# Latent attention: who multiplies the odd items' probabilities by the reciprocals of their sums

## The chip, the cores and the metric

The kernel is one program on one core of a Trainium2 chip. It runs a whole two-block network on 512 tokens of width 1024 in float32. The metric is the device time of one execution in microseconds (us); the median of three executions of the kernel before is 2576.47 us (2576.43 to 2576.89).

## The reference, cut to what matters

The network is a chain of mixers and feed-forward layers. The change touches one of them only, the latent attention (MLA) of the second block, and in it only the softmax:

```python
def chunk_causal_attention(q, k, v):          # q, k: 16 heads of 96, v: 16 heads of 64
    ...
        sc = jnp.einsum('bqhd,bkhd->bhqk', qi, k) * scale
        mask = key_chunk[None, :] <= q_chunk[:, None]
        p = jax.nn.softmax(jnp.where(mask, sc, -jnp.inf), axis=-1)
        return jnp.einsum('bhqk,bkhd->bqhd', p.astype(v.dtype), v)
    ...
```

## The kernel before, in words

Each engine has its own program, and semaphores order them against each other. TensorE runs one long queue of matmuls through the whole network; ScalarE and VectorE prepare operands and read results; GpSimd has little to do.

The latent attention is cut into 32 items (`MLA_ITEMS`). An item is two heads (e = 0, 1) by one block of 128 queries; its width w is the number of keys it sees: 128, 256, 384 or 512 columns. Items come in pairs of one width, an even and an odd one; item m of the pair s = m // 2. By `mla_block` the widths of the pairs 0 to 15 are 128, 256, 384, 512, then 256, 384, 512, 128 three times over. One item goes through these stages, each once for e = 0 and once for e = 1 where it says so:

1. TensorE, `scores` (L2808 and L2813, two matmul lines, both heads): scores into PSUM.
2. VectorE, `maxima` (L2910, once per head): adds the mask, writes the masked scores to SBUF (`mla_soft`) and takes the row maxima; L2917 turns the maxima into the bias of the exponentials and increments `item_max`.
3. ScalarE, `exponentials` (L2883, once per head): the exponentials in place, with their row sums.
4. VectorE, `normed` (L2922, the reciprocals of both sums, then L2924 once per head): probabilities in place, which increments `item_normed`.
5. TensorE, `turn` (L2829): transposes w / 128 blocks of each head into PSUM.
6. ScalarE, `copy` (L2873 or L2876): the transposed probabilities to SBUF.
7. TensorE, `values` (L2844): probabilities times values.

The order on each engine is written out by hand. In step s, TensorE does turn(2s-4), scores of the pair s, turn(2s-3), values(2s-5), values(2s-4) (`pe_mla_step`). VectorE does normed(2s-2), maxima(2s), maxima(2s+1), normed(2s-1) (`dve_mla_soft`), and after that in some steps a piece of other work: two quarter splits of a weight block (L373) in steps 6 and 7, the rope part of a key (two L2738) in steps 7 and 8, the low part of a projection operand (L712) in steps 12 and 14. ScalarE does copy(n-4), exponentials(n-2) (`act_mla_soft`). TensorE may overwrite the score banks of a pair only when the maxima of the pair before are read (the wait for `item_max` in `scores`).

GpSimd's last work before the softmax is `pool_mla` (L2727: 16 additions of squares), its next is `pool_pairs(0)` in the feed-forward layer behind the attention. The statistics (`mla_stat`) of kind 3, the reciprocals, have two slots, one for even and one for odd items.

Of the kernel before, what the change touches and what calls it, by code (L numbers as in the profile page):

```python
# [20 lines left out]
ALU = mybir.AluOpType  # L21
# [136 lines left out]
def build(nc, A, stop=None):  # L158

    with ExitStack() as ctx:  # L160
        sems = {}

        def sem(name):
            if name not in sems:
                sems[name] = ctx.enter_context(nc.semaphore(name))
            return sems[name]
# [2258 lines left out]
        def mla_soft(n, e):  # L2425
            a = (26 + n % 6 * 2 + e) * SEQ
            return arena[:, a:a + SEQ]

        def mla_stat(kind, n, e, count=1):
            c = (4, 12, 20, 24)[kind] + n % (4, 4, 2, 2)[kind] * 2 + e  # L2430
            return stats[:, c:c + count]
# [7 lines left out]
        def k_plain(j, lo=0, hi=P):  # L2439
            return tile(12 + j, lo, hi)  # L2440
# [32 lines left out]
        def pair_squares(s):  # L2473
            return hn_tile(s % 3)
# [243 lines left out]
        def pool_mla(pool):  # L2718

            for s in range(16):  # L2720
# [5 lines left out]
                other = rope_squares(s // 2, s % 2) if s < 8 else krope_sq()  # L2726
                pool.tensor_tensor(pair_squares(s), pair_squares(s), other, ALU.add).then_inc(sem("pair_sq"), 1)  # L2727

        def dve_key(dve, j, parts=("plain", "rope")):
            by = mla_rq(j)  # L2730
            if "plain" in parts:
                dve.wait_ge(sem("head_rsqrt"), j + 1)
                dve.scalar_tensor_tensor(out=k_plain(j), in0=bank[UNIT_BANK[12 + 2 * j]][:, :], scalar=col("kgn"), in1=by,
                                         op0=ALU.mult, op1=ALU.mult).then_inc(sem("key_read"), 1)
            if "rope" in parts:
                for e in range(2):
                    lo = j % 2 * MLA_ROPE + e * HD
                    ins = dve.tensor_tensor(k_rope(j // 2, lo, lo + MLA_ROPE), krope(lo, lo + MLA_ROPE), by[lo:lo + MLA_ROPE, :],  # L2738
                                            ALU.mult)
                ins.then_inc(sem("head_normed"), 1)  # L2740
# [43 lines left out]
        MLA_ITEMS = [mla_item(n) for n in range(32)]  # L2784
# [5 lines left out]
        def pe_mla_step(pe, s):  # L2790
            n0 = len(NA_ITEMS)

            def scores(s):
                g, b = s // 4, mla_block(2 * s)
                w, c = (b + 1) * P, b * P
                if s == 0:
                    pe.wait_ge(sem("pair_read"), 8)
                    pe.wait_ge(sem("q_built"), 4)
                    pe.wait_ge(sem("q_scaled"), 2)
                    pe.wait_ge(sem("proj_read"), 7)  # L2800
                    pe.wait_ge(sem("head_normed"), 5)
                pe.wait_ge(sem("head_normed"), 2 * g + 2)
                for x in range(2):
                    if s:
                        pe.wait_ge(sem("item_max"), n0 + 2 * s - 1 + x)
                    for e in range(2):
                        lo, hi = rows(e)
                        pe.matmul(bank[2 * x + e][:, 0:w], q_plain(2 * g + x, lo, hi)[:, c:c + P],  # L2808
                                  k_plain(2 * g + x, lo, hi)[:, 0:w], start=True, stop=False)
                for x in range(2):  # L2810
                    for e in range(2):
                        lo = x * MLA_ROPE + e * HD
                        pe.matmul(bank[2 * x + e][:, 0:w], q_turned_rope(g, lo, lo + MLA_ROPE)[:, c:c + P],  # L2813
                                  k_rope(g, lo, lo + MLA_ROPE)[:, 0:w], start=False, stop=True).then_inc(sem("item_scored"), 1)

            def turn(n):
                w = MLA_ITEMS[n]["w"]
                if n == 0:
                    pe.wait_ge(sem("proj_read"), 8)
                if n == 1:  # L2820
                    pe.wait_ge(sem("head_rsqrt"), 8)
                both = n and max(w, MLA_ITEMS[n - 1]["w"]) > SEQ // 2
                if n >= 2 or both:
                    pe.wait_ge(sem("item_turned"), n0 + n - 1 + both)
                for e in range(2):
                    pe.wait_ge(sem("item_normed"), 2 * (n0 + n) + e + 1)
                    out, at = turn_at(mla_turn_banks, n, e, w)
                    for c in range(0, w, P):
                        mm = pe.transpose(out[:, at + c:at + c + P], mla_soft(n, e)[:, c:c + P], ident)  # L2829
                mm.then_inc(sem("item_transposed"), 1)  # L2830

            def values(n):
                it, j = MLA_ITEMS[n], n // 8 * 2 + n % 2
                w = it["w"]
                pe.wait_ge(sem("item_turned"), n0 + n + 1)
                if n < 2:
                    pe.wait_ge(sem("proj_read"), 4)
                    pe.wait_ge(sem("key_read"), 7 + n)
                elif n % 8 < 2:
                    pe.wait_ge(sem("mla_out"), j - 1)  # L2840
                for c in range(w // P):
                    for e in range(2):
                        a = e * w + c * P
                        mm = pe.matmul(it["out"][e], it["v"][e][c], mla_turned(n)[:, a:a + P], start=c == 0, stop=c == w // P - 1)  # L2844
                mm.then_inc(sem("item_valued"), 1)

            if 2 <= s <= 17:
                turn(2 * s - 4)
            if s < 16:
                scores(s)  # L2850
            for j, lo, hi in {16: ((0, 0, 2),), 17: ((0, 2, 4),), 18: ((1, 2, 4),)}.get(s, ()):
                pe_row(pe, "mla_o", j, lo, hi)
            if 2 <= s <= 17:
                turn(2 * s - 3)
            if s >= 3:
                values(2 * s - 5)
            if s == 17:
                pe_row(pe, "mla_o", 1, 0, 2)
            if 2 <= s <= 17:
                values(2 * s - 4)  # L2860
# [37 lines left out]
        def dve_mla_soft(dve, part):  # L2898
            n0 = len(NA_ITEMS)

            def maxima(n):
                it = MLA_ITEMS[n]
                w = it["w"]
                if n == 0:
                    dve.wait_ge(sem("q_scaled"), 2)
                if n >= 6:
                    dve.wait_ge(sem("item_transposed"), n0 + n - 5)
                for e in range(2):
                    dve.wait_ge(sem("item_scored"), 2 * (n0 + n) + e + 1)
                    ins = dve.tensor_tensor_reduce(out=mla_soft(n, e)[:, 0:w], in0=it["score"][e], in1=it["bias"][e], scale=1.0,  # L2910
                                                   scalar=NEG, op0=ALU.add, op1=ALU.max, accum_out=mla_stat(2, n, e))
                    if e == 0:
                        ins.then_inc(sem("head_max"), 1)
                    else:
                        dve_order(dve, ins)
                dve.wait_ge(sem("head_max"), n0 + n + 1)
                dve.tensor_tensor(mla_stat(0, n, 0, 2), mla_stat(2, n, 0, 2), it["minus"], ALU.mult).then_inc(sem("item_max"), 1)  # L2917

            def normed(m):
                w = MLA_ITEMS[m]["w"]  # L2920
                dve.wait_ge(sem("item_exp"), 2 * (n0 + m) + 2)
                dve_order(dve, dve.reciprocal(mla_stat(3, m, 0, 2), mla_stat(1, m, 0, 2)))  # L2922
                for e in range(2):
                    dve.tensor_scalar(mla_soft(m, e)[:, 0:w], mla_soft(m, e)[:, 0:w], mla_stat(3, m, e), None, ALU.mult)\  # L2924
                        .then_inc(sem("item_normed"), 1)

            for s in range(*part):
                if s >= 1:
                    normed(2 * s - 2)
                if s < 16:  # L2930
                    maxima(2 * s)
                    maxima(2 * s + 1)
                if s >= 1:
                    normed(2 * s - 1)
                if 6 <= s < 8:
                    for q in range(2):
                        dve_split_quarter(dve, FIRST["mla_o"] + 1, 2 * s - 12 + q)
                if s in (7, 8):
                    dve_key(dve, s - 1, ("rope",))
                if s in (12, 14):  # L2940
                    dve_low_part(dve, "mla_o", At(s // 2 - 6))
# [495 lines left out]
        def _(pool):  # L3437
            for v, c in CONSTS.items():
# [16 lines left out]
            pool.dma_start(arena[:, MLA_T["mmask"]:MLA_T["mmask"] + TABLE_WORDS["mla"]], A["t_mla"])\  # L3455
                .then_inc(sem("tables_loaded"), 16)
            pool_mla(pool)
            pool_pairs(pool, 0)
            pool.wait_ge(sem("w_used"), used(0, "a22", PAIRS - 1))
            pool.dma_start(arena[:, ML_T["stepF"]:ML_T["stepF"] + TABLE_WORDS["step"]], A["t_step"])\  # L3460
# [206 lines left out]
```

## Time and profile before

| | |
|---|---|
| median of three executions | 2576.47 us |
| the profiled execution, its time | 2577.62 us |
| its span in the trace | 2575.8 us |
| granted TensorE clock | 1.00 |
| TensorE busy | 2557.3 us, 99% of the span |
| VectorE busy | 1662.4 us, 65% |
| ScalarE busy | 1276.7 us, 50% |
| GpSimd busy | 360.7 us, 14% |

The time of an execution is the span plus some 1.8 us around it. The ends of matmuls are modelled in the profile, and two that overlap are both counted as busy, so 99% does not say that TensorE works at its peak. The weight load of a matmul (PEld) has an end that is measured; where it was idle and what ended that is told too.

### The profile page before, as it was taken

How to read it: one execution, taken by the hardware profiler on the slowest of the kernel's cores; microseconds unless marked ns; L12 is line 12 of the kernel's file. 1: busy time of each engine (PE TensorE's matmuls, PEld its weight loads, DVE VectorE, ACT ScalarE, POOL GpSimd, SP SyncE). 2: the span in 40 equal slices, each digit the busy share in tenths (PEclk: the TensorE clock that was granted, in tenths of full speed). 3: DMA queues.
4: the chain of work that ended last, by engine and by line, in shares of the span. 5: the costliest groups of instructions: out<-in, count | busy, mean ns of one | idle time of the engine just before them, and what ended most of it. 6: DMA issues, size and time to landing. Idle time of an engine off the chain costs nothing.

```text
span 2575.8 us, 35285 instructions
## 1 busy us (share of the span) xinstructions
PE 2557.3 (99%) x12630; PEld 2030.0 (79%) x12630; DVE 1662.4 (65%) x2398; ACT 1276.7 (50%) x2142; POOL 360.7 (14%) x270
## 2 busy tenths in 40 slices
PE   9999999999999999999999999999999999999999
PEld 7855788888777557888888775799988777899887
DVE  4476677643988895677653778597633546687533
ACT  4326543333546895444333578577533425567432
POOL 0020100000103782100000130000610002000800
PEclk9999999999999999999999999999999999999999
DMA  5330232223243442233222230232232221232222
GB/s 216 106 94 21 91 107 97 92 97 98 82 133 123 131 131 81 72 109 98 96 93 96 95 103 10 65 116 101 89 112 93 96 97 51 97 123 99 82 98 98
DMA packets 74833, 250.44 MB, mean 97 GB/s; under 512 B 8764, under 2 KB 9148, under 8 KB 74336
## 3 DMA queue, kind: packets, MB, share of 16 engines
q1 hardware_dynamic: 73632, 240.63, 28.5%
q0 software_dynamic: 944, 8.33, 0.9%
q8 instruction: 67, 1.10, 0.2%
q14 instruction: 46, 0.38, 0.1%
q10 hardware_dynamic: 144, 0.00, 0.0%
HBM read 242.50 MB, written 2.24 MB: 95 GB/s over the span
## 4 chain that ended last, share of the span: by engine, by line
PE 92%; DVE 3%; ACT 2%; issue 1%; DMA 1%; SPq 0%; POOL 0%; DVEq 0%; ACTq 0%; POOLq 0%
PE bank L432 25%; PE bank L433 24%; PE bank L434 24%; PE bank L1361 2%; PE bank L1363 2%; PE bank L1362 2%; PE bank L2257 2%; PE bank L2808 1%; PE bank L654 1%; PE bank L639 1%; PE bank L3156 1%; PE bank L1706 1%; PE bank L640 1%; PE bank L1695 1%; PE bank L2264 1%
## 5 line engine op out<-in xcount | busy, mean ns | idle before, releaser
L383 DVE TENSOR_TENSOR wlo<-wraw,whi 128x1024 fp32r<-128x1024 f32 x344 | 441.5, 1285 | 448.8 <-ACT whi L360 448.2
L360 ACT ACTIVATE whi<-wraw 128x1024 fp32r<-128x1024 f32 x348 | 366.9, 1056 | 508.5 <-DMA wraw<-in_w 508.3
L432 PE MATMUL bank<-hnhi,whi 128*128 128x512 f32 (+1 forms) x1528 | 596.7, 390 | 1.1 <-DVE wlo L383 0.7
L433 PE MATMUL bank<-hnlo,whi 128*128 128x512 f32 (+1 forms) x1528 | 584.5, 383 | 0.0
L434 PE MATMUL bank<-hnhi,wlo 128*128 128x512 f32 x1392 | 542.1, 389 | 0.0
L432 PE MATMUL bank<-ahi,whi 128*128 128x512 f32 x1184 | 463.5, 391 | 1.9 <-DVE alo L712 1.1
L434 PE MATMUL bank<-ahi,wlo 128*128 128x512 f32 x1184 | 460.8, 389 | 0.0
L433 PE MATMUL bank<-alo,whi 128*128 128x512 f32 x1184 | 460.8, 389 | 0.0
L432 PEld LDWEIGHTS bank<-hnhi,whi 128*128 128x128 f32 x1528 | 287.2, 188 | 86.3 <-issue 29.5
L433 PEld LDWEIGHTS bank<-hnlo,whi 128*128 128x128 f32 x1528 | 287.4, 188 | 57.5 <-issue 3.4
L434 PEld LDWEIGHTS bank<-hnhi,wlo 128*128 128x128 f32 x1392 | 261.3, 188 | 55.7
L432 PEld LDWEIGHTS bank<-ahi,whi 128*128 128x128 f32 x1184 | 222.2, 188 | 53.2 <-DVE alo L712 4.6
L434 PEld LDWEIGHTS bank<-ahi,wlo 128*128 128x128 f32 x1184 | 222.3, 188 | 46.7
L433 PEld LDWEIGHTS bank<-alo,whi 128*128 128x128 f32 x1184 | 222.3, 188 | 45.9 <-issue 0.5
L949 ACT ACTIVATE mT<-mT,cols 128x512 f32<-128x512 f32 x88 | 71.9, 817 | 222.5 <-DVE mT L587 222.5
L906 POOL TENSOR_TENSOR xT<-xT,mT 128x512 f32<-128x512 f32 x20 | 33.9, 1728 | 852.5 <-DVE mT L898 852.5
L712 DVE TENSOR_TENSOR alo<-arena,ahi 128x512 fp32r<-128x512 f32 x140 | 111.0, 793 | 64.5 <-ACT ahi L707 63.8
L707 ACT ACTIVATE ahi<-arena 128x512 fp32r (+1 forms) x140 | 88.2, 632 | 129.2 <-PE bank L434 126.9
L1100 POOL TENSOR_TENSOR arena<-arena,rstd 128x512 f32<-128x512 f32 x64 | 109.8, 1754 | 275.4 <-PE bank L434 275.4
L972 DVE SCALAR_TENSOR_TENSOR mT<-mT,cols 128x511 f32<-128x511 f32 x88 | 66.1, 751 | 98.0 <-ACT mT L949 98.0
L1361 PE MATMUL bank<-tok_hi,whi 128*128 128x256 f32 x312 | 88.6, 284 | 0.4 <-DVE bank L1275 0.4
L1362 PE MATMUL bank<-tok_lo,whi 128*128 128x256 f32 x312 | 88.3, 283 | 0.0
(360 smaller groups left out, 3940.5 us busy)
## 6 DMA issues: line engine op xcount, KB each, us to landing
wraw<-in_w SPq DMA_DIRECT2D x410, 512.0 KB, 3.3
arena<-cs_scratch SPq DMA_DIRECT2D x20, 512.0 KB, 5.9
over_a<-cs_scratch SPq DMA_DIRECT2D x12, 512.0 KB, 6.1
arena<-in_rpb POOLq DMA_DIRECT2D x1, 2880.0 KB, 14.1
arena<-in_t_step POOLq DMA_DIRECT2D x2, 897.0 KB, 5.1
mT<-arena SPq DMA_DIRECT2D x28, 64.0 KB, 2.0
out_dram<-xT SPq DMA_DIRECT2D x7, 256.0 KB, 2.0
arena<-in_t_ab POOLq DMA_DIRECT2D x1, 1472.0 KB, 6.7
```

Source lines behind the costliest of these rows:

```text
L360: act.activation(whi[:, slot * BLOCK:(slot + 1) * BLOCK], wraw[:, slot * BLOCK:(slot + 1) * BLOCK], ACT.Copy).then_inc(sem("w_hi"), 1)
L383: dve.tensor_tensor(low_home(i), wraw[:, slot * BLOCK:(slot + 1) * BLOCK], whi[:, slot * BLOCK:(slot + 1) * BLOCK], ALU.subtract).then_inc ...
L432: pe.matmul(out, wh, ah, start=start, stop=False)
L433: pe.matmul(out, wh, al, start=False, stop=False)
L434: return pe.matmul(out, wl, ah, start=False, stop=stop)
L707: act.activation(ahi[:, c:c + SEQ], src(k), ACT.Copy).then_inc(sem("a_hi"), 1)
L712: dve.tensor_tensor(alo[:, c:c + SEQ], MIXERS[name][0](k), ahi[:, c:c + SEQ], ALU.subtract).then_inc(sem("a_lo"), 1)
L949: act.activation(cbuf(m), ubuf(m), ACT.Identity, bias=col("fb", m + 44 * f), scale=col("fw", m + (132 * f + 44))).then_inc(sem("ffn_center ...
L972: dve.scalar_tensor_tensor(out=c[:, 1:SEQ], in0=u[:, 0:SEQ - 1], scalar=col("fw", m + 132 * f), in1=c[:, 1:SEQ], op0=ALU.mult, op1=ALU.add ...
L1100: pool.tensor_tensor(tile(m), tile(m), rstd[:, :], ALU.mult).then_inc(sem("sum_pool"), 1)
L1361: pe.matmul(out, wh, ah, start=False, stop=False, skip_group_check=True)
L1362: pe.matmul(out, wh, al, start=False, stop=False, skip_group_check=True)
```

## The change

The reciprocals of every item stay on VectorE. For even items nothing else changes. For odd items VectorE no longer does the two multiplications; after the reciprocal it increments `odd_inverse`, and GpSimd, which waits for that, does both multiplications with the same operands and the same operation and increments `odd_normed` after each. TensorE's transposes of an odd item wait for `odd_normed`. From item 3 on VectorE waits, ahead of an odd reciprocal, until GpSimd is done with the odd item before (they share one slot of reciprocals). GpSimd's loop over the 16 odd items stands between `pool_mla` and `pool_pairs(0)`.

```diff
+        def pool_mla_soft(pool):
+
+            for m in range(1, 32, 2):
+                w = MLA_ITEMS[m]["w"]
+                pool.wait_ge(sem("odd_inverse"), m // 2 + 1)
+                for e in range(2):
+                    pool.tensor_scalar(mla_soft(m, e)[:, 0:w], mla_soft(m, e)[:, 0:w], mla_stat(3, m, e), None, ALU.mult)\
+                        .then_inc(sem("odd_normed"), 1)
...
                 for e in range(2):
-                    pe.wait_ge(sem("item_normed"), 2 * (n0 + n) + e + 1)
+                    if n % 2:
+                        pe.wait_ge(sem("odd_normed"), n + e)
+                    else:
+                        pe.wait_ge(sem("item_normed"), 2 * n0 + n + e + 1)
...
             def normed(m):
                 w = MLA_ITEMS[m]["w"]
                 dve.wait_ge(sem("item_exp"), 2 * (n0 + m) + 2)
+                if m % 2:
+                    if m >= 3:
+                        dve.wait_ge(sem("odd_normed"), m - 1)
+                    dve.reciprocal(mla_stat(3, m, 0, 2), mla_stat(1, m, 0, 2)).then_inc(sem("odd_inverse"), 1)
+                    return
                 dve_order(dve, dve.reciprocal(mla_stat(3, m, 0, 2), mla_stat(1, m, 0, 2)))
...
             pool_mla(pool)
+            pool_mla_soft(pool)
             pool_pairs(pool, 0)
```

## Rows read from the trace of the kernel before

**Rows 1.** The page: span, busy time by engine, chain that ended last by engine.
```profile
span 2575.8 us, 35285 instructions
PE 92%; DVE 3%; ACT 2%; issue 1%; DMA 1%; SPq 0%; POOL 0%; DVEq 0%; ACTq 0%; POOLq 0%
```
**Rows 2.** Windows, the softmax stretch (window, length, then busy us of each engine, clock).
```profile
1543.00:1632.00 89.00, 85.20 (x763) 54.46 (x762) 65.09 (x268) 71.04 (x195) 0.77 (x1) 1.00 0.04 13
```
**Rows 3.** Waits, same stretch (engine, line, waited for: us, times, longest).
```profile
DVE stats L2922 <- ACT arena L2883: 12.6, 12, 2.1
...
PEld bank L2808 <- DVE stats L2917: 5.8, 11, 0.8
...
PE bank L432 <- DVE stats L2917: 0.6, 1, 0.6
```
**Rows 4.** Lines by form, same stretch (count, busy us, mean ns, idle before).
```profile
L2924 DVE TENSOR_SCALAR arena<-arena,stats 128x512 f32<-128x512 f32 x16 | 7.1, 484 | 0.3
...
L2924 DVE TENSOR_SCALAR arena<-arena,stats 128x128 f32<-128x128 f32 x16 | 3.9, 283 | 0.3
```
**Rows 5.** GpSimd elsewhere (start us, duration us, operation), then L2727's minimum, median, maximum.
```profile
2113.08 0.61 POOL L3116 COPY arena<-arena 128x512 f32<-128x512 f32 x1 [54.74 <-DVE arena L3315]
2115.99 1.00 POOL L3119 TENSOR_TENSOR arena<-arena 128x384 f32<-128x384 f32 x1 [2.29 <-DVE arena L3315]
2122.24 0.46 POOL L3119 TENSOR_TENSOR arena<-arena 128x128 f32<-128x128 f32 x1 [3.65 <-DVE arena L3315]
...
L2727 POOL TENSOR_TENSOR over_hn<-over_hn x8: 1257/1292/1922, 1486.8 to 1515.1; 128x512 f32<-128x512 f32 x8
```
**Rows 6.** Timeline, item 11 (384 columns), and the next transposes' weight load.
```profile
1575.23 0.16 DVE L2922 RECIPROCAL stats<-stats 128x2 f32<-128x2 f32 x1
1575.42 0.75 DVE L2924 TENSOR_SCALAR arena<-arena,stats 128x384 f32<-128x384 f32 x2
...
1576.09 0.76 DVE L373 TENSOR_TENSOR wlo<-wraw,whi 128x256 fp32r<-128x256 f32 x2
1576.22 0.87 PE L2829 MATMUL bank<-base_t,arena 128*128 128x128 f32 x6
...
1578.48 0.86 PEld L2829 LDWEIGHTS bank<-base_t,arena 128*128 128x128 f32 x8 [0.38 <-ACT arena L2876]
```
**Rows 7.** Timeline, item 13 (512 columns) and what VectorE and TensorE do behind it.
```profile
1580.02 0.17 DVE L2922 RECIPROCAL stats<-stats 128x2 f32<-128x2 f32 x1
1580.22 0.88 DVE L2924 TENSOR_SCALAR arena<-arena,stats 128x512 f32<-128x512 f32 x2
...
1581.02 0.75 DVE L373 TENSOR_TENSOR wlo<-wraw,whi 128x256 fp32r<-128x256 f32 x2
...
1581.37 1.09 PE L2829 MATMUL bank<-base_t,arena 128*128 128x128 f32 x8
1581.69 1.37 DVE L2738 TENSOR_TENSOR arena<-over_a,sq 32x512 f32<-32x512 f32 x2
...
1583.09 0.17 DVE L2922 RECIPROCAL stats<-stats 128x2 f32<-128x2 f32 x1
...
1584.80 1.76 PE L2808 MATMUL bank<-arena 64*128 64x384 f32 x8 [0.29 <-DVE stats L2917]
```
**Rows 8.** Timeline, VectorE's other work behind item 27, and a weight load in pair 10's scores.
```profile
1616.75 0.69 DVE L712 TENSOR_TENSOR alo<-over_hn,ahi 128x512 fp32r<-128x512 f32 x1
...
1590.84 0.30 PEld L2808 LDWEIGHTS bank<-arena 64*128 64x128 f32 x4 [0.81 <-DVE stats L2917]
```
**Rows 9.** Timeline, VectorE beside GpSimd in the projections just before the softmax.
```profile
1537.94 2.50 DVE L2738 TENSOR_TENSOR arena<-over_a,sq 32x512 f32<-32x512 f32 x2
1538.61 1.29 POOL L2727 TENSOR_TENSOR over_hn<-over_hn,over_a 128x512 f32<-128x512 f32 x1 [2.33 <-ACT over_hn L2670]
...
1542.23 1.54 POOL L2727 TENSOR_TENSOR over_hn<-over_hn,over_a 128x512 f32<-128x512 f32 x1 [2.33 <-ACT over_hn L2670]
1543.59 0.29 DVE L2910 CUSTOM_DVE_ANT_0 arena<-bank,arena 128x128 f32<-128x128 f32 x1 [0.94 <-PE bank L2813]
```

## The prediction

> **What bounds the kernel now.** I read the page first. TensorE carries 92% of the chain that ended last, VectorE 3%, GpSimd nothing [rows 1]. So the end moves only by what TensorE's queue gains or loses. The change touches one stretch of 89 us; there TensorE shows 85.2 us busy, ScalarE 71.0, VectorE 65.1, GpSimd 0.8, at a full clock [rows 2]. VectorE has 24 us to spare in it and isn't the bound.
>
> Then I read the waits of that stretch [rows 3], for they hold all that a faster VectorE could give back. TensorE's weight loads of the scores wait 5.8 us in 11 places for L2917, the last step of the maxima, and the first matmul of the output projection waits 0.6 us: 6.4 us at most, part of it the usual pace of the loads. On the other side VectorE itself waits 12.6 us, 12 times, for exponentials. In the timeline 11 of these 12 waits stand ahead of an even item's reciprocals, the first thing of a step, and the twelfth ahead of item 31's. This decides most of the case: what VectorE saves at the end of a step by leaving out an odd item's multiplications, it then waits longer at the start of the next, because the exponentials come when they come. The maxima behind them start no earlier, nor do the scores.
>
> **Part one, what is taken from VectorE.** 32 of the 64 multiplications go. A pair costs 0.88 us at 512 columns and 0.75 at 384 [rows 6, 7], some 2 x 0.283 = 0.57 at 128 [rows 4]: together about 11 us of VectorE's time. It counts only where no wait of VectorE follows. By the timeline the even reciprocals that follow without one are those of items 2, 14, 16 and 18. Behind 18 the maxima wait for scores anyway. So the savings of items 1 (0.57), 13 (0.88) and 15 (0.57) can reach TensorE: 2.0 us is the most that this part brings. TensorE is indeed held there, 0.29 us before the scores behind item 14, and the load behind item 16 shows 0.81 us of idle [rows 7, 8]. From 1580.02 to 1583.09 VectorE goes without a pause through reciprocals, multiplications, two L373 and two L2738 to the next reciprocals [rows 7].
>
> **Part two, what GpSimd takes for it.** No row shows a multiplication by a per-partition scalar on GpSimd, so I bound it. Below: the copy of 128x512, also one tensor in and one out, 0.61 us. Above: the operations with two tensors in, 1.29 us at 512 columns, 1.00 at 384, 0.46 at 128 [rows 5]. From the last two a column costs 0.27 us per 128 and the start 0.19; with the same start the copy costs 0.105 per 128, thus 0.51 at 384 and 0.30 at 128 (estimates). I take the copy's price, because the multiplication has the copy's traffic of one tensor in and one out, and the scalar is one value per partition. In the timeline GpSimd's copy began 0.08 us after the end of the VectorE operation that it waited for.
>
> The new wait stands in TensorE's queue in front of the transposes of an odd item, and behind it all of TensorE's work. What matters is when the second head is ready, against the moment at which TensorE reaches its transposes. The tightest items are those of 384 and 512 columns:
> - Item 11 (384). TensorE starts at 1576.22 and reaches the second head after three transposes of 0.13, at 1576.61. GpSimd alone would be done at 1575.39 + 0.08 + 2 x 0.51 = 1576.49, 0.12 in time [rows 6]. Items 19 and 27 stand the same way.
> - Item 13 (512). TensorE needs the second head at 1581.37 + 4 x 0.13 = 1581.89; GpSimd alone is done at 1580.19 + 0.08 + 2 x 0.61 = 1581.49, 0.40 in time [rows 7]. Items 21 and 29 likewise.
> - In the first four pairs, at 128 and at 256 columns TensorE comes at least half a us later than it needs to; GpSimd adds under 0.4. Nothing is lost.
> So at the copy's price GpSimd is slower than VectorE by 0.1 to 0.4 us an item, and the cover, TensorE's scores ahead of the transposes, just holds.
>
> **Part three, the two engines beside each other.** An L2738 pair took 2.50 us when a GpSimd operation of 1.29 ran beside it, 1.37 without one [rows 7, 9]: the operations waited for each other by about a whole operation (2.50 - 1.37 = 1.13). The maxima did not: L2910 took 0.29 us inside a GpSimd operation, its usual time at 128 columns [rows 9]. Where VectorE waits for exponentials behind an odd reciprocal, GpSimd has the memory to itself. Where work with two SBUF operands follows, it does not:
> - Item 11: two L373 (0.38 each). One between GpSimd's two operations makes it 1576.87, both 1577.25: TensorE stalls 0.26 to 0.64, I take 0.4. Behind it TensorE's load waits 0.38 us for ScalarE anyway [rows 6], so about 0.2 is left.
> - Item 13: L373 twice, then L2738 twice. If all take turns, GpSimd ends at 1582.24 (0.35 late), and VectorE reaches item 14 at 1580.19 + 0.75 + 1.37 + 1.22 = 1583.53, 0.44 later than now, instead of 0.88 earlier [rows 7]. The two delays lie over each other: 0.4. The 0.88 of part one is gone.
> - Item 15: 0.57 saved, 0.6 of GpSimd's time beside L2738: nothing either way.
> - Item 27: L712 of 0.69 [rows 8] puts GpSimd 0.57 late; the ScalarE wait of 0.4 and the 0.6 us at the output projection [rows 3] absorb it.
> Sum: 0.2 + 0.4, less 0.1 for item 1 where the maxima come earlier and TensorE was barely waiting: +0.5 us. Bounds: -2.0 if nothing interferes, +1.5 if none of these stalls is absorbed (0.64 + 0.44 + 0.57, less 0.1).
>
> The Trainium skill speaks against such a split. Its page "SBUF — State Buffer", section "Who interferes with whom", says that VectorE operations with two SBUF inputs and GpSimd operations that read SBUF exclude each other for a whole instruction, and that VectorE's fast two-port forms, a tensor_scalar among them, do so too. The trace agrees on the first with the 2.50 against 1.37 us above. By the second the even items' multiplications collide as well; no row here shows it, and only item 17 has one close behind, in front of a wait of VectorE's.
>
> **What else is added.** VectorE's wait for GpSimd's odd item before: that item's multiplications ended a whole step (some 5 us) earlier, so it costs nothing, and behind it would be queued the reciprocal and the next step's maxima. On GpSimd the loop delays `pool_pairs(0)`, whose first operation comes some 50 us after the last item. `pool_mla` is done at 1543.77 [rows 9], before the first odd reciprocal. No DMA is issued by either.
>
> **Rivals.**
> - *GpSimd's multiplication costs what its two-tensor operations cost.* Then a 384-column item is ready 0.16 + 0.08 + 2.00 = 2.24 us after its reciprocal starts and is needed after 1.38 (1576.61 - 1575.23): 0.86 late. A 512-column one is ready after 2.83 and needed after 1.87: 0.96 late. Three of each (items 11, 19, 27; 13, 21, 29) make 5.5 us, the collisions add 1.5, and waits absorb some 2: +5 us, 2581.5 (2580 to 2584). It decides against the change from about 0.57 us an operation at 384 columns. For it: the only rows of arithmetic on GpSimd are at that price. Against it: they read two tensors. Chance 0.15.
> - *A price between the two*, 0.75 at 384 and 0.92 at 512: 384 columns 0.36 late, 512 columns 0.2 late, three times each, 1.7, and collisions 1.5, less 1 absorbed: +2.2 us, 2578.7. Chance 0.18. The Trainium skill's "GPSIMD Engine Reference", section "Elementwise — side-by-side cycle accounting", has 1.03 cycles an element for bodies of up to two operations and some 1.8 (769 ns for 512 elements) for a tight loop of more; the copy's row lies at the former, and a multiplication at the latter would be this rival.
> - *The relief arrives.* GpSimd finds gaps, VectorE's collisions cost nothing, and items 1, 13 and 15 give back most of 2.0 us: 2575.0. For it: VectorE is on the path from 1580 to 1585. Against: rows 9. Chance 0.12.
> - *The change turns out to do nothing where it counts*, which is the forecast: VectorE's time is swapped for its own waiting, and small collisions remain. Chance 0.55.
>
> **How the numbers follow.** The sum is made against the profiled execution, 2577.62 us (span 2575.8 us and 1.8 around it), which lies 1.15 above the median of 2576.47; with +0.5 it would be 2578.1, and the median 2577.0. The range takes in the relief and the middle price and ends inside the first rival: 2575.0 to 2580.5. A measurement here can tell about 0.2%, 5.2 us, from no change. Faster by that isn't possible by part one, save by what I have overlooked: 0.02. Slower by it needs the upper half of the first rival: 0.08. Same: 0.90.
>
> **What would show it.** VectorE's busy time in the stretch falls by about 11 us and its waits for L2883 grow by nearly as much. GpSimd shows 32 operations, 0.61 us at 512 columns; a value near 0.9 or 1.3 names the rival. L373 and L2738 behind item 13 should be longer, and the reciprocals of item 14 come no earlier than now in relation to those of 13. TensorE's transposes of items 11, 13 and 27 should show short waits for GpSimd, the others none. The forecast is wrong if TensorE waits for GpSimd at most odd items, or if the maxima get longer beside GpSimd.

## The result and the profile after

The kernel after takes 2588.98 us (median of five, 2588.03 to 2589.41) against 2576.51 us for the kernel before: +12.5 us, a ratio of 1.0046, 95% interval 1.0034 to 1.0057. Run a second time beside other kernels it took 2588.40 against 2577.23: 1.0043, 1.0029 to 1.0056. So it is slower by 11 to 12.5 us, outside my range of 2575.0 to 2580.5 and on the side to which I had given 0.08.

The page of after, its first rows and two of its chain:

```profile
span 2586.5 us, 35300 instructions
...
PE 2561.0 (99%) x12630; PEld 2032.8 (79%) x12630; DVE 1655.2 (64%) x2366; ACT 1276.1 (49%) x2142; POOL 397.7 (15%) x302
...
PE 92%; DVE 3%; ACT 2%; POOL 1%; issue 1%; DMA 1%; SPq 0%; DVEq 0%; ACTq 0%; POOLq 0%
PE bank L432 25%; PE bank L433 24%; PE bank L434 24%; PE bank L1361 2%; PE bank L1363 2%; PE bank L1362 2%; PE bank L2257 2%; POOL arena L2735 1%; PE bank L654 1%; PE bank L639 1%; PE bank L3173 1%; PE bank L1706 1%; PE bank L640 1%; PE bank L1695 1%; PE bank L2264 1%
```

The span grew by 10.7 us, and GpSimd, which had 0% of the chain [rows 1], now has 1%, by one line: L2735, the new multiplication. (The change shifts lines: L2841 is the transposes, L2856 the values, L2817 and L2822 the scores, L2885 and L2888 ScalarE's copies, L2895 the exponentials, L2937 the odd reciprocals, L2939 the even ones, L2941 the even items' multiplications.) GpSimd's instructions by shape (count, busy us, mean ns of one, idle before):

```profile
L2735 POOL TENSOR_SCALAR arena<-arena,stats 128x512 f32<-128x512 f32 x8 | 13.1, 1650 | 13.5 <-DVE stats L2937 13.5
L2735 POOL TENSOR_SCALAR arena<-arena,stats 128x384 f32<-128x384 f32 x8 | 10.8, 1358 | 15.9 <-DVE stats L2937 15.9
L2735 POOL TENSOR_SCALAR arena<-arena,stats 128x256 f32<-128x256 f32 x8 | 7.3, 924 | 12.4 <-DVE stats L2937 12.4
L2735 POOL TENSOR_SCALAR arena<-arena,stats 128x128 f32<-128x128 f32 x8 | 5.9, 740 | 15.1 <-DVE stats L2937 15.1
```

I had put these at 0.61 and 0.51 us for 512 and 384 columns. The waits from 1535 to 1650 us show who pays (engine, line, waited for: us in total, times, longest):

```profile
DVE stats L2939 <- ACT arena L2895: 22.5, 13, 3.3
ACT arena L2888 <- PE bank L2841: 13.4, 10, 2.2
...
DVE stats L2937 <- ACT arena L2895: 9.4, 8, 3.4
...
PE bank L2841 <- POOL arena L2735: 8.5, 12, 1.0
...
PEld bank L2841 <- POOL arena L2735: 6.7, 8, 1.1
```

TensorE's transposes wait for GpSimd, 8.5 us by its matmuls; where these show no idle, a weight load may. VectorE saves its multiplications and waits longer for exponentials: 22.5 + 9.4 = 31.9 us against 12.6 [rows 3]. ScalarE, in turn, waits 13.4 us for the transposes before its copies of 384 and 512 columns, where the kernel before has 1.8:

```profile
ACT arena L2876 <- PE bank L2829: 1.8, 3, 0.8
```

One tight item in the timeline of after, item 19 (start us, duration us, engine and operation, idle before):

```profile
1601.16 2.47 POOL L2735 TENSOR_SCALAR arena<-arena,stats 128x384 f32<-128x384 f32 x2 [4.25 <-DVE stats L2937]
1602.52 0.31 PEld L2841 LDWEIGHTS bank<-base_t,arena 128*128 128x128 f32 x3 [1.12 <-issue]
1602.55 0.52 PE L2841 MATMUL bank<-base_t,arena 128*128 128x128 f32 x3 [0.96 <-POOL arena L2735]
1603.67 0.31 PEld L2841 LDWEIGHTS bank<-base_t,arena 128*128 128x128 f32 x3 [0.85 <-POOL arena L2735]
1603.68 0.55 PE L2841 MATMUL bank<-base_t,arena 128*128 128x128 f32 x3 [0.61 <-POOL arena L2735]
```

TensorE stands idle 0.96 us before the transposes of the first head and another 0.61 before those of the second. The block x6 of 0.87 us that one saw before [rows 6] is cut in two.

The reciprocals of the odd items show where the time goes, pair by pair (by the timelines, each distance within one trace). From item 1's to item 31's it is 76.03 us before and 86.92 in after, 10.89 more, as much as the span grew. The distances behind items 11, 13, 19, 21, 27 and 29 grew by 8.25 together (1.05 to 1.66 each), those behind 5 and 7 by 1.24 and 0.97, the other seven by 0.43 together. From item 31's reciprocals to the end of the network it is 0.3 us more.

### The profile page after: what moved, and what is told of

The parts are those of the page before. It is cut to its first block, busy times and chain, and to the rows that moved or that the text cites. A ratio compares the mean times of both kernels' runs of the same rounds, so it can differ in the third digit from the quotient of the medians.

```text
span 2586.5 us, 35300 instructions
## 1 busy us (share of the span) xinstructions
PE 2561.0 (99%) x12630; PEld 2032.8 (79%) x12630; DVE 1655.2 (64%) x2366; ACT 1276.1 (49%) x2142; POOL 397.7 (15%) x302
## 4 chain that ended last, share of the span: by engine, by line
PE 92%; DVE 3%; ACT 2%; POOL 1%; issue 1%; DMA 1%; SPq 0%; DVEq 0%; ACTq 0%; POOLq 0%
PE bank L432 25%; PE bank L433 24%; PE bank L434 24%; PE bank L1361 2%; PE bank L1363 2%; PE bank L1362 2%; PE bank L2257 2%; POOL arena L2735 1%; PE bank L654 1%; PE bank L639 1%; PE bank L3173 1%; PE bank L1706 1%; PE bank L640 1%; PE bank L1695 1%; PE bank L2264 1%
## 5 line engine op out<-in xcount | busy, mean ns | idle before, releaser
L712 DVE TENSOR_TENSOR alo<-arena,ahi 128x512 fp32r<-128x512 f32 x140 | 111.5, 796 | 68.3 <-ACT ahi L707 68.2
```

The lines of the kernel that those rows point to most:

```text
L712: dve.tensor_tensor(alo[:, c:c + SEQ], MIXERS[name][0](k), ahi[:, c:c + SEQ], ALU.subtract).then_inc(sem("a_lo"), 1)
```

## The experiments

Each kernel was timed in five rounds against the kernel before, run beside it; differences are between those medians. The intervals of these ratios are 0.09 to 0.14% to each side, 2.3 to 3.6 us, so a difference of one us is a hint and not a finding. The distance from the first to the last odd reciprocals, one trace of each kernel, leaves out the scatter of the rest of the network:

| kernel | us between the medians | first to last odd reciprocals, us |
|---|---|---|
| before | | 76.03 |
| VectorE's other work moved | -1.2 | 75.02 |
| nobody multiplies | -1.0 | 75.20 |
| GpSimd copies | -0.7 | 75.44 |
| 128 and 256 columns only | +0.1 | 75.83 |
| one head each | +1.7 | 77.45 |
| items 19 and 21 | +2.8 | 78.72 |
| items 11 and 13 | +2.9 | 78.72 |
| double copy | +7.8 | 83.12 |
| values first | +10.5 | 86.83 |
| both waits filled | +11.0 | 87.02 |
| five more transposes | +11.5 | 87.91 |
| after | +12.5 | 86.92 |
| after again | +11.2 | 88.27 |

**GpSimd copies instead of multiplying.**

```diff
-pool.tensor_scalar(mla_soft(m, e)[:, 0:w], mla_soft(m, e)[:, 0:w], mla_stat(3, m, e), None, ALU.mult)
+pool.tensor_copy(mla_soft(m, e)[:, 0:w], mla_soft(m, e)[:, 0:w])
```

> The kernel after, but GpSimd copies each odd item's probabilities in place instead of multiplying them: as many GpSimd operations on the same tiles, and the odd items stay unscaled, so that part of the computation is left out. Price theory (the 12.5 us are the price of one GpSimd multiplication, about 1.24 us at 384 columns and 1.56 at 512 in the trace of after, against the 0.51 and 0.61 that I assumed from the copy): with the copy's price the blind sum holds and the time is before + 0.5 us, between -1 and +2. Collision theory (GpSimd and VectorE exclude each other, whatever GpSimd does): most of the loss stays, at least before + 6 us.

2575.06 us against 2575.78: -0.7 us (ratio 0.9997, 0.9988 to 1.0006). The same 32 operations on the same tiles, behind the same waits, cost nothing. Only their duration differs. GpSimd in its timeline, items 19 and 21, then item 13, which has VectorE's L373 and L2738 (here L2747) beside it:

```profile
1594.86 0.96 POOL L2735 COPY arena<-arena 128x384 f32<-128x384 f32 x2 [5.04 <-DVE stats L2937]
1599.27 1.17 POOL L2735 COPY arena<-arena 128x512 f32<-128x512 f32 x2 [3.46 <-DVE stats L2937]
...
1578.85 1.15 DVE L373 TENSOR_TENSOR wlo<-wraw,whi 128x256 fp32r<-128x256 f32 x2
1578.99 1.48 POOL L2735 COPY arena<-arena 128x512 f32<-128x512 f32 x2 [3.52 <-DVE stats L2937]
...
1579.92 1.78 DVE L2747 TENSOR_TENSOR arena<-over_a,sq 32x512 f32<-32x512 f32 x2
```

A pair took 0.96 us at 384 columns and 1.17 at 512, which confirms what I interpolated for copies (2 x 0.51, 2 x 0.61) and that these durations fit under TensorE's scores. The price theory holds, and as the cause of the 12 us the collision theory falls. Collisions there are: at item 13 VectorE's two pairs took 1.15 and 1.78 us where they had taken 0.75 and 1.37 [rows 7].

**Nobody multiplies the odd items.**

```diff
             def normed(m):
+                if m % 2:
+                    dve.reciprocal(mla_stat(3, m, 0, 2), mla_stat(1, m, 0, 2)).then_inc(sem("item_normed"), 2)
+                    return
```

> The kernel before, but nobody multiplies the odd items; VectorE still makes their reciprocals (the scaling of odd items is left out). It measures by itself what the relief of VectorE can bring. Swap theory (the relief ends in VectorE's own waits for the exponentials): before - 0.5 us, and by no more than the 2.0 us of the blind bound; VectorE's waits for L2883 grow from 12.6 us to over 20. Relief theory (VectorE is a hidden bound): more than 2 us faster.

2574.79 against 2575.78: -1.0 us (the same interval, 0.9988 to 1.0006, which holds no change). This is all that relieving VectorE can bring, and a GpSimd that cost nothing would bring no more. VectorE's waits for the exponentials:

```profile
DVE stats L2925 <- ACT arena L2883: 19.9, 12, 2.3
...
DVE stats L2923 <- ACT arena L2883: 2.4, 2, 2.2
```

22.3 us against 12.6 [rows 3]: for some 10.7 us less work (54.38 us busy in the stretch of [rows 2] instead of 65.09) VectorE waits 9.7 more. The swap is as forecast.

**GpSimd takes only 128 and 256 columns.** The loop runs over items 1, 3, 9, 15, 17, 23, 25, 31:

```diff
-            for m in range(1, 32, 2):
+            for k, m in enumerate(MLA_POOLED):
```

> GpSimd multiplies only the odd items of 128 and 256 columns (8 of 16), VectorE the others. Price theory: two multiplications of 0.92 us at 256 columns end 2.1 us after the reciprocals begin, TensorE comes 2.3 us or more after; two of 0.60 at 128 end 1.4 after, TensorE comes 1.8 after (items 1, 15, 23) and about 1.0 after for item 31: no stall but that of item 31, before + 0.5 us (0 to +1.5). Collision theory: GpSimd's time beside L2738 and L712 behind items 15 and 23 shows, before + 2 us or more.

2575.85 against 2575.78: +0.1 us (0.9991 to 1.0009). Half of the items moved, nothing lost; TensorE comes to them later than GpSimd is done. The mean of GpSimd's multiplication at 256 columns was 922 ns.

**One head each.**

```diff
-                for e in range(2):
+                for e in (1,):
                     pool.tensor_scalar(mla_soft(m, e)[:, 0:w], mla_soft(m, e)[:, 0:w], mla_stat(3, m, e), None, ALU.mult)
...
+                    dve.tensor_scalar(mla_soft(m, 0)[:, 0:w], mla_soft(m, 0)[:, 0:w], mla_stat(3, m, 0), None, ALU.mult)
```

> Of every odd item VectorE multiplies the first head and GpSimd the second. Price theory: one multiplication ends 0.24 + 1.24 = 1.48 us after the reciprocals begin at 384 columns and is needed after 1.38; at 512 it is 1.80 against 1.87: stalls of 0.1 us in three or four items, before + 0.5 us (0 to +2). If the loss were per item moved, and not per late end, half of it would stay: before + 6 us.

2577.45 against 2575.78: +1.7 us (1.0006, 0.9997 to 1.0015; the distance of the reciprocals grew by 1.4). All 16 odd items are still on GpSimd's path and a seventh of the loss is left, so it isn't per item. It is somewhat over my 0.5 because GpSimd's operation became longer beside VectorE's multiplication of the other head:

```profile
1557.59 0.42 DVE L2939 TENSOR_SCALAR arena<-arena,stats 128x384 f32<-128x384 f32 x1
1557.64 1.47 POOL L2735 TENSOR_SCALAR arena<-arena,stats 128x384 f32<-128x384 f32 x1 [4.27 <-DVE stats L2937]
```

1.47 instead of 1.24 us (the next kernel has 1.24 by itself); with L373 or L712 beside it as well it took 1.72 at item 11 and 1.99 at item 27, and behind these two the distances grew by 0.32 and 0.58 us. The Trainium skill, "SBUF — State Buffer", section "Who interferes with whom", says that VectorE's tensor_scalar can, in its two-port form, block GpSimd for the whole instruction. The trace agrees in kind and not in size: VectorE's operation overlapped GpSimd's by 0.37 us and delayed it by 0.23.

**Two items, without and with VectorE's other work beside them.** The same edit as above with `MLA_POOLED = [19, 21]`, and with `[11, 13]`: the same widths, 384 and 512.

> GpSimd multiplies items 19 (384 columns) and 21 (512) only, behind which VectorE has nothing but its wait for exponentials. Price theory: item 19 is late by 0.24 + 2 x 1.24 - 1.38 = 1.34 us, item 21 by 0.24 + 2 x 1.56 - 1.87 = 1.49; TensorE's waits for ScalarE behind each take back some 0.2: before + 2.3 us (1.5 to 3).

> GpSimd multiplies items 11 (384 columns) and 13 (512) only: the widths of the last kernel, but with L373 and L2738 of VectorE, two SBUF operands each, right behind the reciprocals. Price theory alone: the same time as with items 19 and 21, within 0.5 us. With collisions on top: slower than that one by the 0.4 to 1.5 us of L373 and L2738 that stand between, and GpSimd's operations at item 13 longer than 1.56 us.

2579.82 and 2579.84 against 2576.98: +2.84 and +2.86 us (both 1.0011, 1.0002 to 1.002). The lateness worked out from the single durations was 1.34 + 1.49 = 2.83. GpSimd's operations, first without and then with L373 and L2738 beside them:

```profile
L2737 POOL TENSOR_SCALAR arena<-arena,stats 128x512 f32<-128x512 f32 x2 | 3.1, 1562 | 3.4 <-DVE stats L2940 3.4
L2737 POOL TENSOR_SCALAR arena<-arena,stats 128x384 f32<-128x384 f32 x2 | 2.5, 1239 | 52.5 <-DVE stats L2940 52.5
```

```profile
L2737 POOL TENSOR_SCALAR arena<-arena,stats 128x512 f32<-128x512 f32 x2 | 3.7, 1860 | 3.4 <-DVE stats L2940 3.4
L2737 POOL TENSOR_SCALAR arena<-arena,stats 128x384 f32<-128x384 f32 x2 | 2.8, 1411 | 31.7 <-DVE stats L2940 31.7
```

The collisions are real, 0.30 and 0.17 us an operation. That the two times are equal doesn't show them to be free. The reciprocals of the odd item, of the next and of the one behind, first with items 19 and 21, then with 11 and 13:

```profile
1596.93 0.16 DVE L2940 RECIPROCAL stats<-stats 128x2 f32<-128x2 f32 x1
1602.79 0.17 DVE L2940 RECIPROCAL stats<-stats 128x2 f32<-128x2 f32 x1 [1.06 <-ACT arena L2897]
1608.96 0.17 DVE L2942 RECIPROCAL stats<-stats 128x2 f32<-128x2 f32 x1 [1.60 <-ACT arena L2897]
```

```profile
1575.32 0.16 DVE L2940 RECIPROCAL stats<-stats 128x2 f32<-128x2 f32 x1
1581.52 0.17 DVE L2940 RECIPROCAL stats<-stats 128x2 f32<-128x2 f32 x1 [1.17 <-ACT arena L2897]
1588.29 0.17 DVE L2942 RECIPROCAL stats<-stats 128x2 f32<-128x2 f32 x1 [1.60 <-ACT arena L2897]
```

The distances are 5.86 and 6.17 us without VectorE's other work and 6.20 and 6.77 with it: 0.34 and 0.60 more, which is by how much GpSimd's pairs are longer (2.82 against 2.47, 3.70 against 3.10). The collisions count in full. But the kernel before has 4.79 and 4.54 at items 19 and 21 and 4.79 and 5.48 at 11 and 13: there VectorE's own unbroken work [rows 7] held the next items back by 0.94, and GpSimd's lateness covers that. 0.94 lost by the collisions and 0.94 that was lost before anyway make the two totals equal, which is a coincidence of sizes.

**Double the copy.** In the kernel with copies each copy is followed by a second one of the same tile, behind a wait for the first.

```diff
+                    pool.tensor_copy(mla_soft(m, e)[:, 0:w], mla_soft(m, e)[:, 0:w]).then_inc(sem("pair_sq"), 1)
+                    pool.wait_ge(sem("pair_sq"), 16 + m + e)
                     pool.tensor_copy(mla_soft(m, e)[:, 0:w], mla_soft(m, e)[:, 0:w])
```

> The kernel after with two copies on GpSimd in place of each multiplication, one behind the other (the scaling of odd items is left out). By the durations of the single copies (0.48 at 384 columns, 0.59 at 512, and some 0.1 for the wait between) a head takes 1.06 us at 384 and 1.28 at 512. Price theory by the blind rule: a 384-column item is ready after 0.24 + 2.12 = 2.36 us, 0.98 late; a 512-column one after 2.80, 0.93 late; six of them 5.7, less some 1 to 2 absorbed: before + 4 to + 5 us, between the single copy (-0.7) and the multiplication (+12). Collision theory: twice as many operations for VectorE to collide with, so more than + 8.

2585.01 against 2577.23: +7.8 us (1.0029, 1.0018 to 1.0040), between the two theories' numbers. The duration again makes the loss: -0.7 us at 2 x 0.51 and 2 x 0.61, +7.8 at 2 x 1.05 and 2 x 1.26 (by the starts and ends in its timeline), +11.2 at 2 x 1.24 and 2 x 1.56. My 4 to 5 us were too few. The lateness of the six items adds up to 5.5 (0.95 and 0.89 each), items 5 and 7 add 0.5 and 0.2, and nothing of these 6.3 us was absorbed. By the reciprocals the growth is 5.8, 0.9, and 0.4 at the rest, 7.1 in all; the remaining 0.7 lies outside this stretch.

**TensorE kept busy while it waits.** The first of these kernels has five more transposes at each odd item of 384 or 512 columns. By its edit they stand behind the wait for the first head and ahead of that head's own transposes, and not between the heads as I wrote. The second has six of constants ahead of the wait for the first head and five ahead of the wait for the second. The edit of the second:

```diff
+                        for c in range((6, 5)[e] if w > SEQ // 2 else 0):
+                            pe.transpose(bank[mla_turn_banks(n)[e]][:, 0:P], ones, ident)
                         pe.wait_ge(sem("odd_normed"), n + e)
```

> The kernel after, with five more transposes (0.13 us each) on TensorE between the two heads of every odd item of 384 or 512 columns, where it stands idle 0.4 to 0.9 us for GpSimd anyway; they write a bank that the second head's transposes overwrite. Clock theory (part of the loss is TensorE's clock, which fell to half speed for some 4 us behind items 11 and 21 in the trace of after): the clock stays at 1.00 and the time is after - 1.5 to - 3 us, 2586 to 2587. Without it: after + 0 to + 1 us, 2588 to 2590.

> The kernel after, with TensorE kept busy in both of its waits at odd items of 384 and 512 columns: six transposes of constants ahead of the wait for the first head (0.77 us; it stood idle 0.1 to 1.0), five ahead of the second (0.64 us; idle 0.4 to 0.8). Five alone, between the heads, had left the clock falling (0.74 and 0.66 of full speed in two stretches) behind the idle of 0.9 before the first. Clock theory: now the clock stays at 1.00, and the time falls by what the two slow stretches cost, some 1.5 to 3 us under the kernel after. If it stays as it was, the clock's loss was hidden behind the waits for GpSimd.

The first took 2588.49 us against 2576.98 (+11.5), and the clock still fell, so it settled nothing. The second took 2588.22 against 2588.40 for the kernel after beside it: no difference that can be told from scatter. The third column from the right is the granted clock, first from after, then from the second of these kernels (each window with its length and the busy times of TensorE, its weight loads, VectorE, ScalarE and GpSimd):

```profile
1580.00:1585.00 5.00, 4.81 (x35) 4.13 (x37) 3.75 (x16) 2.82 (x7) 1.62 (x2) 0.66 0.00 0
...
1605.00:1610.00 5.00, 5.00 (x38) 3.63 (x35) 0.70 (x6) 3.57 (x11) 3.00 (x2) 0.70 0.02 3
```

```profile
1580.00:1585.00 5.00, 4.88 (x52) 3.64 (x52) 3.76 (x16) 4.27 (x12) 1.62 (x2) 1.00 0.00 0
...
1605.00:1610.00 5.00, 4.94 (x47) 3.66 (x43) 2.00 (x12) 4.11 (x12) 3.04 (x2) 1.00 0.00 0
```

In after the clock stood at its lower level for part of two windows (behind items 11 and 19; what I had expected of the first kernel names 21); a window's 0.66 and 0.70 are means over both levels. With TensorE busy it stays at 1.00, and nothing is gained: the reciprocals behind items 11, 13, 19 and 21 are 6.20, 6.76, 5.85 and 6.17 us apart against 6.20, 6.76, 5.84 and 6.20 in after. The slow stretches fell into time in which TensorE would have waited for the next GpSimd result anyway. As an account of the 12 us the clock theory falls.

Beside it the kernel after itself ran again:

> The kernel after itself, beside the others on the same chip: before + 12 us (11 to 13).

2588.40 against 2577.23: +11.2 us. Its profiled execution, the longest of its five with 2589.86 us, shows that the clock isn't always free. There it fell early enough to slow the transposes of the second head, at items 5 and 27:

```profile
1561.78 0.83 PE L2841 MATMUL bank<-base_t,arena 128*128 128x128 f32 x3 [0.82 <-POOL arena L2735]
1627.32 0.90 PE L2841 MATMUL bank<-base_t,arena 128*128 128x128 f32 x3 [0.61 <-POOL arena L2735]
```

In after both blocks took 0.55 us, and the distances to the next odd reciprocals are longer here by just these 0.28 and 0.35 us; with 0.24 behind item 7 and 0.48 behind item 29 this execution takes 1.35 us more than after's between the first and last odd reciprocals. The first of the two kernels with more transposes shows the same: its clock fell in the transposes of item 19, and the next odd reciprocals came 6.52 us later instead of 5.84.

**Values ahead of the odd transposes.** TensorE does the values of the pair before while GpSimd is at work.

```diff
-            if 2 <= s <= 17:
-                turn(2 * s - 3)
             if s >= 3:
                 values(2 * s - 5)
+            if 2 <= s <= 17:
+                turn(2 * s - 3)
```

> The kernel after, with TensorE's values of the odd item of the pair before moved ahead of the transposes of the odd item, so that TensorE comes to GpSimd's result later and works meanwhile. By the trace the moved values take 0.5 us (8 records of 0.06) ahead of a 384-column item and 0.75 (12) ahead of a 512-column one. Late-end theory (what counts is only how far GpSimd's second operation ends behind TensorE's arrival): of 1.34 and 1.49 us of lateness 0.84 and 0.74 are left in each of the six late items, 4.7 us, with items 5 and 7 about 0.5 more: before + 5 to + 7 us instead of + 12. If instead the later ScalarE copies and exponentials carry the loss from pair to pair whatever TensorE does meanwhile: before + 10 us or more.

2586.47 against 2575.93: +10.5 us (1.0040, 1.0027 to 1.0054). TensorE's waits for GpSimd became a little shorter (6.8 us by the matmuls instead of 8.5), the stretch from the first to the last odd reciprocals not at all: 86.83 us against 86.92. This is the case that I had set against the late-end theory: something carries the loss from pair to pair whatever TensorE does meanwhile. The chain that ended last in this kernel, item 19 to item 21, shows what (start us, duration us, piece):

```profile
1599.96 0.18 DVE stats L2937
1600.14 0.08 issue
1600.22 2.47 POOL arena L2735 x2
1602.69 0.04 issue
1602.74 0.56 PE bank L2841 x3
1603.30 0.02 issue
1603.33 0.83 ACT arena L2888 x2
1604.16 0.63 issue
1604.79 0.63 ACT arena L2895 x2
...
1605.81 0.18 DVE stats L2937
1605.99 0.08 issue
1606.07 3.12 POOL arena L2735 x2
```

It is a loop over all four engines. The reciprocals of item 19 release GpSimd; its two multiplications release the transposes; these release ScalarE's copy of item 19; and in ScalarE's order the exponentials of item 21 stand behind that copy, and they release the reciprocals of item 21. From one reciprocal to the next it is 5.85 us. Before, by the timeline, the reciprocals of these two items were 4.79 us apart, with the copies on GpSimd 4.42, and in after 5.84. Moving TensorE's work about doesn't shorten a loop in which TensorE has 0.56 us.

**No GpSimd, VectorE's other work moved.**

```diff
-                if s in (7, 8):
-                    dve_key(dve, s - 1, ("rope",))
+                if s in (4, 5):
+                    dve_key(dve, s + 2, ("rope",))
```

> No GpSimd: the kernel before, with the two pairs of L2738 of VectorE moved from behind steps 7 and 8 to behind steps 4 and 5, where VectorE waits 1.36 and 1.26 us for exponentials and the pair takes 1.37. If VectorE's time counts only where it doesn't wait, as I hold, this gives more than the whole relief by GpSimd could: before - 0.8 us (-1.5 to -0.3). If VectorE's time counts nowhere: before, within 0.3.

2575.82 against 2576.98: -1.2 us (0.9995, 0.9985 to 1.0004; 11 runs of 2575.06 to 2576.77 beside 27 of 2576.15 to 2578.99). The interval holds no change, so it isn't shown to be faster; its median has the size that was expected, and the wait of 0.29 us ahead of the scores behind item 14 [rows 7] is gone:

```profile
1583.93 1.56 PE L2808 MATMUL bank<-arena 64*128 64x384 f32 x8
```

It moves four instructions and gives as much as leaving out 32 did, by the reciprocals too (75.02 and 75.20 us against 76.03).

## Why the prediction was wrong

**What failed.** One step: the price of GpSimd's multiplication. I took the copy's, "because the multiplication has the copy's traffic of one tensor in and one out". The chip has 1.24 us at 384 columns instead of 0.51, and 1.56 at 512 instead of 0.61. That is above my upper bound too (1.00 and 1.29, from operations with two tensors in): the bounds were drawn from the number of operands, and neither held. With the measured price my own lines on items 11 and 13 give what happened: 0.24 + 2 x 1.24 = 2.72 us against a need after 1.38, 1.34 late; 0.24 + 2 x 1.56 = 3.36 against 1.87, 1.49 late. Two items cost 2.84 us on the chip for these 2.83. Three of each are 8.5. Items 5 and 7, which I had called safe because GpSimd "adds under 0.4", are late by 0.9 and 0.8 with this price (5: 2.72 against 1.80; 7: 3.36 against 2.54, by the timeline of before). That makes 10.2 us of the span's 10.7 and of the 11.2 and 12.5 us of the two comparisons. By the reciprocals in after the six cost 8.25 and these two 2.2; the collisions are in these figures, partly hidden as with items 11 and 13 above.

**The forecast's logic with the right price for it.** The kernel with copies is that forecast, executed: +0.5 us foretold, -0.7 measured, with an interval that holds both; the trace tells more. What was off there is part three. For item 11 I had 0.2 of collisions after what is absorbed; the distance to the next odd reciprocals is 4.79 us as before. For item 13 I took off the whole relief and added 0.4: the relief was indeed taken off (5.38 us against 5.48 before and 4.55 where nobody multiplies; 0.4 each is what L373 and L2747 lost beside the copies), but the 0.4 on top didn't come. For item 15 I had "nothing either way", and it brought the gain: 4.69 us against 5.20.

**The relief.** Right: at most 2.0 us by the bound, 1.0 measured with nobody doing the work, and VectorE's waits grew by nearly what it saved.

**The first rival.** It had the mechanism, TensorE stopped at the transposes of items 11, 13, 19, 21, 27 and 29, and the right side of its threshold of 0.57 us at 384 columns. Its size was too small three times: by the price, by "waits absorb some 2", and by leaving out items 5 and 7. The double copy, near this rival's price, measured +7.8 where it said +5. (The second rival's price, 0.75 and 0.92 us, was lower still.) The waits for ScalarE that I wanted to absorb delays with aren't slack. ScalarE's copy waits for the very transposes that are late, and its exponentials stand behind the copy, so a late end is handed on to the next odd reciprocals. I had written that the exponentials "come when they come"; they come behind the copy.

**The chances.** I gave 0.90 to no change on an assumption for which no row of arithmetic with a scalar stood, and 0.08 to what came. At 384 and 512 columns all rows of arithmetic on GpSimd lay above the threshold of 0.57 us, and the copy's estimate of 0.51 barely below it. That should have weighed more than an argument about traffic.

**The signs that I named.** At 512 columns "a value near 0.9 or 1.3 names the rival": it showed 1.65 in the mean, beyond both. Transposes waiting for GpSimd at most odd items: 12 waits by matmuls and 8 by weight loads. VectorE's busy time over the span fell by 7.2 us, not by 11: its 32 multiplications that are left took 12.7 us where they had taken 11.0, and the first L2738 pair (here L2747) 1.8 instead of 1.4. The maxima didn't get longer, 688 ns against 689 at 512 columns.

## What to carry to other kernels

Before an operation moves to another engine, find a row of that operation on that engine; the number of its operands doesn't give the price, and where no row exists the range has to reach to what every arithmetic row there costs and beyond. Add what the operation loses beside the work that runs next to it (item 13's pair took 3.70 us instead of 3.10). Compare twice that price with the time from release to need, here 1.38 us at the tightest item: under it the move is free (copies, narrow items), over it every item pays the difference. And relief for an engine that waits for another anyway returns as more waiting: look at what stands right behind the freed work.

## What the runs showed of the hardware

- GpSimd's multiplication of a float32 tile by a per-partition scalar took 598 ns at 128 columns at the least, 922 at 256, 1239 at 384 and 1562 at 512 when undisturbed: 0.32 us per 128 columns, longer than the addition of two tensors (1.29 us at 512 [rows 5]) and 2.5 times the copy.

```profile
L2735 POOL TENSOR_SCALAR arena<-arena,stats x32: 598/1167/1911, 1549.2 to 1636.7; 128x128 f32<-128x128 f32 x8, 128x256 f32<-128x256 f32 x8, 128x384 f32<-128x384 f32 x8, 128x512 f32<-128x512 f32 x8
```

- VectorE's plain multiplication and GpSimd's delay each other, though each has one tensor in. In after, the even item 6's pair beside a GpSimd operation took 1.12 us where it had taken 0.88 [rows 7 for the same width]:

```profile
1560.65 1.12 DVE L2941 TENSOR_SCALAR arena<-arena,stats 128x512 f32<-128x512 f32 x2
```

- TensorE's clock fell to the lower of its two levels (1.2 GHz) behind waits of 0.94 to 0.96 and 0.61 us close together at items 11 and 19 of after, and those slow stretches cost no time in the end. The same waits don't always bring it down: at item 27 of after (0.95 and 0.61) and at item 11 of the kernel with items 11 and 13 alone (0.93 and 0.62) it stayed at 1.00, and when after ran again it stayed at 1.00 behind items 11 and 19 and fell at items 5 and 27. When it falls before the second head's transposes are done, it costs what they lose, 0.28 and 0.35 us there.
